# The unit matrix of a chunk's transition: added by the tensor engine in the accumulation, with the copy-out on the scalar engine

## The chip, the cores and the metric

One core of a Trainium2 chip runs the whole program. The metric is the device time of one execution in microseconds (us). PE is the tensor engine, DVE the vector engine, ACT the scalar engine, POOL the general one, SP the one that issues most loads; each has its own queue of instructions and they meet only at semaphores.

## What is computed

The reference is one layer of a streaming encoder over 512 prompt tokens and 32 sample tokens. One of its two mixing branches is a scan with a 64x64 matrix state for each of 8 heads:

```python
def step(s, inp):
    r_t, d_t, k_t, v_t, kk_t, b_t = inp
    sa = jnp.einsum('bhvk,bhk->bhv', s, -kk_t)
    s = (s * d_t[:, :, None, :] + sa[..., None] * b_t[:, :, None, :]
         + v_t[..., None] * k_t[:, :, None, :])
    return s, jnp.einsum('bhvk,bhk->bhv', s, r_t)
```

The kernel doesn't step token by token. For a chunk of 64 tokens (32 for the sample) the state goes over as a matrix product, S_new = (S E + update), scaled by the decay at the chunk's end. E = I + (a 64x64 product of two token-by-64 matrices) is the chunk's transition, and this case is about how its I comes in.

## The kernel before

All matrix products are in f32. The large projections ("dense", line 892) are cut into blocks of 128 output columns; each step of a block is three products (high and low parts of weights and activations), each over two halves of 272 tokens, into one of two PSUM buffers dense0 and dense1. The order of all work is one list, `SCHEDULE`; every engine walks through it and does its own share of each step, so that each engine's order is the list's order.

The scan runs over 5 tiles t: four of 128 tokens (two chunks each) and, as t = SAMPLE = 4, one of 32 tokens (one chunk). A tile is done for two groups g of four heads; c is the pair of heads, p the half of the 128 partitions that a head of the pair has. Small results share a ring of four PSUM banks, side0 to side3: the n-th filling takes bank n % 4, and PE may start it only when the filling four before it has been drained (`open_bank`, `drained`).

In a tile the steps that matter here are, in order of the list: `wu` (PE, line 818; ACT copies the result to `wu`, line 1275), `e` (PE, line 829; DVE adds I and writes `ebd`, line 1638), one piece of dense work of 12 products as filler, and then the next tile's triangular inversion (`wt` line 944 with ACT's copy to `xt` at 1285, `wm` line 744, `wd` line 758), woven with this tile's state update (`chain0` and `chain1`, lines 839, 840 and 844, which read `ebd`; DVE drains them to `mbd`, line 1646) and with the last tile's normalisation (line 1064 and others). In the sample's tile the filler between `wu` and `e` is a piece too. The gate filler of some tiles ends a block; then ACT applies tanh from dense0 or dense1 to `gst` (line 1401) and issues a store (line 1404). The tanh needs another ACT table than the square root at line 1318, so there is a table load where the two alternate.

Step `e` before: for each chunk one bank is filled by four products, one per head, `wu` transposed times `tok`; a bank is a 2x2 arrangement of 64x64 results. With K = 64 rows (the chunk's tokens) and 64 columns each product uses a quarter of PE's array: the rows of partitions 0-63 or 64-127 by the chunk, the columns 0-63 or 64-127 by p. In the sample's tile the products have K = 32.

DVE drains a bank with two instructions, one for each half of the partitions, each 64 partitions by 128 elements, with the unit matrix of the constants (`cst`, columns K_I64 on) as second operand of the addition.

Of the kernel before, what the change touches and what calls it, by code (L numbers as in the profile page):

```python
# [14 lines left out]
P = 128  # L15
# [329 lines left out]
def encoder_kernel(nc, i_, o_):  # L345
# [225 lines left out]
    def chunks(t):  # L571
        return [(c, CHUNK) for c in range(2)] if t < SAMPLE else [(0, DEC)]
# [158 lines left out]
    def wkv_pe(pe, step, transposes, close):  # L731
# [41 lines left out]
        if st == "tok":  # L773
            transposes(step, "t0", [((2 * q + c) * P, C[:, blk + 2 * g + c, 1 + j0:1 + j0 + n])
                                    for q, blk in enumerate((CR, CK)) for c in range(2)])
            transposes(step, "t1", [(c * P, C[:, CV + 2 * g + c, 1 + j0:1 + j0 + n]) for c in range(2)]
                       + [((2 + c) * P, AR[:, 2 * g + c, 0, j0:j0 + n]) for c in range(2)])
        elif st == "sb0":
            if t == 0:
                pe.wait_ge(s_["rw_done"], 2 * g + 2)  # L780
            w = 2 * B32 if nb > 1 else B32
            for p in range(2):
                b = open_bank(pe, step, f"b{p}")
                lo, hi = 64 * p, 64 * p + 64
                for c in range(2):
                    for q in range(nb):
                        i0 = j0 + 32 * q
                        ins = pe.matmul(b[32 * q:32 * q + 32, c * 64:c * 64 + w], C[lo:hi, CR + 2 * g + c, 1 + i0:1 + i0 + B32],
                                        AR[lo:hi, 2 * g + c, 0, i0:i0 + w], start=True, stop=True)
                close(ins, step, f"b{p}")  # L790
        elif st in ("sb1", "sk"):
            f, blk, us = ("r", CR, slice(1, 2)) if st == "sb1" else ("k", CK, slice(0, 2))
            m = n * (us.stop - us.start)
            for p in range(2):
                b = open_bank(pe, step, f"{f}{p}")
                lo, hi = 64 * p, 64 * p + 64
                for c in range(2):
                    ins = pe.matmul(b[0:n, c * m:(c + 1) * m].rearrange("p (u i) -> p u i", i=n),  # L798
                                    C[lo:hi, blk + 2 * g + c, 1 + j0:1 + j0 + n], AR[lo:hi, 2 * g + c, us, j0:j0 + n],
                                    start=True, stop=True)  # L800
                close(ins, step, f"{f}{p}")
        elif st == "gv":
            b = open_bank(pe, step, "gv")
            landed(pe, ("w", "tok", t, g), "t1")
            landed(pe, ("w", "sk", t, g), "k0")
            landed(pe, ("w", "sk", t, g), "k1")
            for h in range(4):
                ins = pe.matmul(b[0:n, h * 64:(h + 1) * 64], gt[0:n, g, h, 0:n], tok[0:n, g, 2, h, :], start=True, stop=True)  # L808
            close(ins, step, "gv")
        elif st == "wu":  # L810
            b = open_bank(pe, step, "wu")
            if nb > 1:
                landed(pe, ("wd", last_lv, t, g), "d")
            else:
                pe.wait_ge(s_["x64_set"], g + 1)
            landed(pe, ("w", "gv", t, g), "gv")
            for h in range(4):
                ins = pe.matmul(b[0:n, h * P:(h + 1) * P], xt64[0:n, g, h, 0:n],  # L818
                                ag[0:n, g, h, :, :].rearrange("p u v -> p (u v)"), start=True, stop=True)
            close(ins, step, "wu")  # L820
        elif st == "e":
            landed(pe, ("w", "wu", t, g), "wu")
            landed(pe, ("w", "tok", t, g), "t0")
            for ch, ln in chunks(t):
                b = open_bank(pe, step, f"e{ch}")
                r0, r1 = 64 * ch, 64 * ch + ln
                for c, p in heads:
                    h = 2 * c + p
                    ins = pe.matmul(b[64 * p:64 * p + 64, c * 64:(c + 1) * 64], wu[r0:r1, g, h, 0, :], tok[r0:r1, g, 0, h, :],
                                    start=True, stop=True)  # L830
                close(ins, step, f"e{ch}")
        elif st in ("chain0", "chain1"):
            ch = int(st[-1])
            r0, r1 = 64 * ch, 64 * ch + chunks(t)[ch][1]
            b = open_bank(pe, step, "c")
            for c, p in heads:
                h = 2 * c + p
                out = b[64 * p:64 * p + 64, c * P + 64 * p:c * P + 64 * p + 64]
                pe.matmul(out, tok[r0:r1, g, 0, h, :], wu[r0:r1, g, h, 1, :], start=c == 0, stop=False, skip_group_check=c > 0)  # L839
                pe.matmul(out, tok[r0:r1, g, 1, h, :], tok[r0:r1, g, 2, h, :], start=False, stop=True, skip_group_check=c > 0)  # L840
            landed(pe, ("w", "e", t, g), f"e{ch}")
            state_landed(pe, t, ch, g)
            for c in range(2):
                ins = pe.matmul(b[:, c * P:(c + 1) * P], ebd[:, g, ch, c, :], mbd[:, g, ch, c, :], start=False, stop=True,  # L844
                                skip_group_check=True)
            close(ins, step, "c")
        elif st == "q":
            b = open_bank(pe, step, "q")
            for p in range(2):
                landed(pe, ("w", "sb1", t, g), f"r{p}")  # L850
            for c, p in heads:
                h = 2 * c + p
                ins = pe.matmul(b[64 * p:64 * p + 64, c * n:(c + 1) * n], wu[0:n, g, h, 0, :], rb[0:n, g, h, 0:n],
                                start=True, stop=True)
            close(ins, step, "q")
        elif st == "ya":


            b = open_bank(pe, ("w", "yb", t, g), "y")
            for c, p in heads:  # L860
                h = 2 * c + p
                out = b[64 * p:64 * p + 64, c * n:(c + 1) * n]
                pe.matmul(out, wu[0:n, g, h, 1, :], rb[0:n, g, h, 0:n], start=c == 0, stop=False,
                          skip_group_check=c > 0)
                pe.matmul(out, tok[0:n, g, 2, h, :], gt[0:n, g, h, P:P + n], start=False, stop=True,
                          skip_group_check=c > 0)
        elif st == "yb":

            b = bank(step, "y")
            landed(pe, ("w", "q", t, g), "q")  # L870
            for ch, ln in chunks(t):
                state_landed(pe, t, ch, g)
                for c in range(2):
                    ins = pe.matmul(b[:, c * n + 64 * ch:c * n + 64 * ch + ln], mbd[:, g, ch, c, :],  # L874
                                    qT[:, g, c, 64 * ch:64 * ch + ln], start=False, stop=True, skip_group_check=True)
            close(ins, step, "y")
# [222 lines left out]
    def _(act):  # L1099
# [19 lines left out]
        for step in SCHEDULE:  # L1119
# [141 lines left out]
            elif k == "w":  # L1261
# [8 lines left out]
                elif st == "gv":  # L1270
                    b = full_bank(act, step, "gv")
                    drain(f_act(ag[0:n, g, :, 1, :], b[0:n, 0:256].rearrange("p (h v) -> p h v", h=4), ACT.Copy), step, "gv")
                elif st == "wu":
                    b = full_bank(act, step, "wu")
                    drain(f_act(wu[0:n, g, :, :, :].rearrange("p h u v -> p (h u v)"), b[0:n, 0:512], ACT.Copy, scale=-1.0),
                          step, "wu")
                elif st == "yb":
                    b = full_bank(act, step, "y")
                    drain(f_act(AR[:, 2 * g:2 * g + 2, 1, j0:j0 + n], b[:, 0:2 * n].rearrange("p (c i) -> p c i", c=2),
                                ACT.Copy), step, "y")  # L1280
# [148 lines left out]
    def _(dve):  # L1429
# [27 lines left out]
        for step in SCHEDULE:  # L1457
# [146 lines left out]
            elif k == "w":  # L1604
# [19 lines left out]
                elif st == "sk":  # L1624
                    mask = cst[0:n, K_SC:K_SC + 2 * P].rearrange("p (u i) -> p u i", u=2)[:, :, 0:n]
                    mask = mask.unsqueeze(1).broadcast_to([n, 2, 2, n])
                    for p in range(2):
# [1 line left out]
                        o = gt[0:n, g, p::2, :].rearrange("p c (u i) -> p c u i", u=2)[:, :, :, 0:n]  # L1629
                        drain(vec.tensor_tensor(o, b[0:n, 0:4 * n].rearrange("p (c u i) -> p c u i", c=2, u=2), mask,  # L1630
                                                ALU.mult), step, f"k{p}")
                elif st == "e":
                    for ch, ln in chunks(t):
                        b = full_bank(dve, step, f"e{ch}")
                        for p in range(2):
                            lo, hi = 64 * p, 64 * p + 64
                            i64 = cst[lo:hi, K_I64:K_I64 + 64].unsqueeze(1).broadcast_to([64, 2, 64])
                            ins = vec.tensor_tensor(ebd[lo:hi, g, ch, :, lo:hi], b[lo:hi, 0:P].rearrange("p (c k) -> p c k", c=2),
                                                    i64, ALU.add)
                        drain(ins, step, f"e{ch}")  # L1640
                elif st in ("chain0", "chain1"):

                    ch = int(st[-1])
# [196 lines left out]
```

## Time and profile before

| | |
|---|---|
| time before, median of 3 runs | 1107.36 us (1107.15 to 1109.85) |
| the profiled execution | 1107.29 us, of which the trace's span is 1105.5 us |
| PE busy | 1011.3 us, 91% of the span |
| DVE / ACT / POOL busy | 501.0 / 276.5 / 490.8 us |
| mean granted PE clock | 0.969 of full speed |

The scan with its fillers lies between about 355 and 565 us; before it are the input projections and attention, after it the output projections and the feed-forward part, which PE fills almost without a gap. The profile counts an f32 product as two weight loads (PEld) and two matmuls (PE), so that "x16" at line 829 is eight products. The form "64*64" beside a matmul is rows by columns of the array that its weights take. Matmuls overlap in the record: a group's duration reaches to the end of its last one, and the next group may have begun by then.

### The profile page before, as it was taken

The page shows a single profiled execution, that of the slowest core. Times are in us where ns is not written, and L with a number is a line of the kernel's source. Part 1 is how long each engine was busy: PE and PEld are TensorE (multiplying, and loading weights), DVE is VectorE, ACT ScalarE, POOL GpSimd, SP SyncE. Part 2 cuts the span into 40 slices and gives each one's busy share as a digit, 9 for nine tenths or more (in the row PEclk, how much of TensorE's full clock was granted, in tenths as well). Part 3 has the DMA queues.
Part 4 walks back from the last instruction along what each step waited for, and adds up shares of the span by engine and source line. Part 5 has one row for each costly group of instructions (what it writes and reads, how often), then busy time and mean ns, then how long its engine had stood idle before and what let it go on. Part 6 is the DMA issues. An engine that isn't in the chain of part 4 may idle for free.

```text
span 1105.5 us, 21747 instructions
## 1 busy us (share of the span) xinstructions
PE 1011.3 (91%) x8886; PEld 954.9 (86%) x8886; DVE 501.0 (45%) x859; ACT 276.5 (25%) x768; POOL 490.8 (44%) x327
## 2 busy tenths in 40 slices
PE   4999998899958889989989994999999999999995
PEld 4999998887856777768789994999999999999994
DVE  5566798367565555554348317232332333200003
ACT  4223452255421222423221235110110111010111
POOL 3555564323233113142164550555655556556561
PEclk9999999999979999999999996999999999999997
DMA  8233323422212100002412531233232332332232
GB/s 240 72 90 83 77 77 97 120 59 70 78 60 60 35 2 31 31 13 75 156 49 71 183 95 39 58 94 88 83 95 77 94 89 81 88 89 85 74 86 82
DMA packets 137580, 89.15 MB, mean 81 GB/s; under 512 B 5242, under 2 KB 129504, under 8 KB 137504
## 3 DMA queue, kind: packets, MB, share of 16 engines
q1 hardware_dynamic: 128356, 70.42, 22.5%
q10 hardware_dynamic: 9148, 17.65, 4.5%
q8 instruction: 56, 0.92, 0.4%
q14 instruction: 20, 0.16, 0.0%
HBM read 78.86 MB, written 9.19 MB: 80 GB/s over the span
## 4 chain that ended last, share of the span: by engine, by line
PE 80%; DVE 12%; ACT 2%; issue 2%; POOL 1%; DMA 1%; DVEq 0%; ACTq 0%; POOLq 0%
PE dense L892 64%; PE side L944 4%; PE side L844 1%; PE side L818 1%; PE side L1064 1%; PE side L987 1%; PE side L874 1%; PE side L808 1%; PE side L1013 1%; DVE amax L1509 1%; DVE mb L1803 1%; PE side L839 1%; PE side L798 1%; DVE gain L1452 1%; DVE otok L1536 1%
## 5 line engine op out<-in xcount | busy, mean ns | idle before, releaser
L647 POOL TENSOR_SCALAR w_hi<-w_raw 128x1024 fp32r<-128x1024 f32 x127 | 139.2, 1096 | 484.5 <-PE dense L892 467.0
L650 POOL TENSOR_TENSOR w_lo<-w_raw,w_hi 128x1024 fp32r<-128x1024 f32 x127 | 311.7, 2455 | 10.6
L892 PE MATMUL dense<-h_hi,w_hi 128*128 128x272 f32 x1392 | 306.3, 298 | 10.1 <-DVE h_lo L1445 8.5
L892 PE MATMUL dense<-h_lo,w_hi 128*128 128x272 f32 x1392 | 296.1, 290 | 0.0
L892 PE MATMUL dense<-h_hi,w_lo 128*128 128x272 f32 x1392 | 294.9, 289 | 0.0
L892 PEld LDWEIGHTS dense<-h_hi,w_hi 128*128 128x128 f32 x1392 | 222.9, 191 | 20.1 <-DVE h_lo L1445 9.6
L892 PEld LDWEIGHTS dense<-h_lo,w_hi 128*128 128x128 f32 x1392 | 224.3, 191 | 0.0
L892 PEld LDWEIGHTS dense<-h_hi,w_lo 128*128 128x128 f32 x1392 | 223.4, 191 | 0.0
L892 PE MATMUL dense<-S,w_hi 128*128 128x272 f32 x960 | 162.0, 291 | 1.7 <-DVE S L1806 1.5
L892 PEld LDWEIGHTS dense<-S,w_hi 128*128 128x128 f32 x960 | 136.5, 189 | 2.5 <-DVE S L1806 2.0
L892 PE MATMUL dense<-S,w_lo 128*128 128x272 f32 x480 | 99.5, 289 | 0.0
L1720 DVE TENSOR_TENSOR z<-side,gain 128x512 f32<-128x512 f32 x16 | 11.1, 692 | 175.2 <-ACT h_lo L1332 175.2
L892 PEld LDWEIGHTS dense<-S,w_lo 128*128 128x128 f32 x480 | 75.5, 188 | 0.0
L1777 DVE SCALAR_TENSOR_TENSOR S<-z,S 128x544 f32 (+1 forms) x22 | 53.7, 2442 | 22.4 <-ACT S L1371 22.4
L1772 DVE TENSOR_TENSOR z<-z,dense 128x544 f32<-128x544 f32 x22 | 15.9, 722 | 97.1 <-PE dense L892 97.1
L1421 ACT ACTIVATE zT<-dense 128x544 f32<-128x544 f32 x16 | 10.0, 625 | 157.0 <-PE side L944 134.8
L1371 ACT ACTIVATE S<-z 128x544 f32 (+1 forms) x22 | 14.5, 658 | 132.2 <-DVE z L1772 132.2
L1768 DVE SCALAR_TENSOR_TENSOR z<-z,dense 128x544 f32<-128x544 f32 x22 | 15.9, 721 | 58.7 <-ACT z L1367 58.7
L1367 ACT ACTIVATE z<-dense 128x544 f32<-128x544 f32 x22 | 13.7, 624 | 99.6 <-PE dense L892 99.6
L1167 ACT ACTIVATE qkv<-side,amax 128x128 f32<-128x128 f32 (+4 forms) x40 | 20.0, 500 | 42.3 <-DVE amax L1510 41.2
L704 POOL TENSOR_TENSOR AR<-AR 128x256 f32<-128x256 f32 (+1 forms) x10 | 6.9, 685 | 44.0 <-DVE AR L1697 44.0
L1658 DVE TENSOR_TENSOR gain<-side,cst 128x256 f32<-128x256 f32 (+1 forms) x40 | 13.5, 376 | 21.1 <-PE side L744 21.0
(249 smaller groups left out, 1314.9 us busy)
## 6 DMA issues: line engine op xcount, KB each, us to landing
w_raw<-in_w_ffn_in SPq DMA_DIRECT2D x44, 512.0 KB, 3.8
w_raw<-in_w_in SPq DMA_DIRECT2D x43, 512.0 KB, 3.9
w_raw<-in_w_ffn_out SPq DMA_DIRECT2D x16, 448.0 KB, 3.6
gates<-gst ACTq DMA_DIRECT2D x16, 272.0 KB, 2.0
w_raw<-in_w_o SPq DMA_DIRECT2D x8, 512.0 KB, 3.8
w_raw<-in_w_ffn_out SPq DMA_DIRECT2D x8, 512.0 KB, 3.7
mb<-gates ACTq DMA_DIRECT2D x1, 2176.0 KB, 8.8
ga<-gates ACTq DMA_DIRECT2D x1, 2176.0 KB, 9.4
```

Of the source, the lines that this page charges most:

```text
L647: nc.gpsimd.tensor_scalar(w_hi[:, slot, :], w_raw[:, slot, :], 1.0, 0.0, ALU.mult, ALU.add).then_inc(hi_split, 1)
L650: nc.gpsimd.tensor_tensor(w_lo[:, slot, :], w_raw[:, slot, :], w_hi[:, slot, :].bitcast(F32), ALU.subtract).then_inc(w_split, 1)
L892: ins = pe.matmul(acc[:, hf, 0:HALF], w, r[:, hf * HALF:(hf + 1) * HALF], start=first and n == 0, stop=final and n == 2)
L944: ins = pe.transpose(b[0:m, c0:c0 + n], src, ident[0:n, 0:n])
L1167: drain(f_act(probs[0:n, pb, m, 0:keys], b[0:n, 0:keys], ACT.Exp, bias=amax[0:n, 2 * pb + m:2 * pb + m + 1], scale=SCALE, accum_out=asum[0 ...
L1367: f_act(f_t.rearrange("p (a b) -> p a b", a=2), pa[:, :, 0:HALF], ACT.Tanh, scale=0.5).then_inc(s_["f_tanh"], 1)
L1371: f_act(dst, f_s.unsqueeze(1), ACT.Copy, scale=0.5).then_inc(s_["f_hi"], 1)
L1658: drain(vec.tensor_tensor(mce[:, g, 0:nb, :].rearrange("p b (h j) -> p b h j", h=4), src, mask.unsqueeze(1).broadcast_to([P, nb, 4, 16]), ...
L1720: drain(vec.tensor_tensor(z[:, 0:4, i * P:(i + 1) * P], bank(step, "z0")[:, 0:512].rearrange("p (t n) -> p t n", t=4), gi.unsqueeze(1).bro ...
L1768: vec.scalar_tensor_tensor(out=fs2, in0=ft2, scalar=1.0, in1=dps[sa][:, :, 0:HALF], op0=ALU.add, op1=ALU.mult).then_inc(dense_read[sa], 1)
L1772: vec.tensor_tensor(fs2, fs2, dps[sb_][:, :, 0:HALF], ALU.mult).then_inc(dense_read[sb_], 1)
L1777: vec.scalar_tensor_tensor(out=lo, in0=f_s.unsqueeze(1), scalar=0.5, in1=hi.bitcast(F32), op0=ALU.mult, op1=ALU.subtract).then_inc(s_["f_l ...
```

## The change

Step `e` only. On PE each of the four products of a bank is now preceded by a product of the unit matrix with itself into the same 64x64 place (start=True), and the old product accumulates on it (start=False). ACT copies the bank to `ebd` with two plain copies of 64 partitions by 128 elements; DVE has no part in the step any more.

```diff
                 for c, p in heads:
                     h = 2 * c + p
-                    ins = pe.matmul(b[64 * p:64 * p + 64, c * 64:(c + 1) * 64], wu[r0:r1, g, h, 0, :], tok[r0:r1, g, 0, h, :],
-                                    start=True, stop=True)
+                    out = b[64 * p:64 * p + 64, c * 64:(c + 1) * 64]
+                    i64 = cst[64 * ch:64 * ch + 64, K_I64:K_I64 + 64]
+                    pe.matmul(out, i64, i64, start=True, stop=False)
+                    ins = pe.matmul(out, wu[r0:r1, g, h, 0, :], tok[r0:r1, g, 0, h, :], start=False, stop=True)
                 close(ins, step, f"e{ch}")
...
+                elif st == "e":
+                    for ch, ln in chunks(t):
+                        b = full_bank(act, step, f"e{ch}")
+                        for p in range(2):
+                            lo, hi = 64 * p, 64 * p + 64
+                            ins = f_act(ebd[lo:hi, g, ch, :, lo:hi], b[lo:hi, 0:P].rearrange("p (c k) -> p c k", c=2), ACT.Copy)
+                        drain(ins, step, f"e{ch}")
...
-                elif st == "e":
-                    for ch, ln in chunks(t):
-                        b = full_bank(dve, step, f"e{ch}")
-                        for p in range(2):
-                            lo, hi = 64 * p, 64 * p + 64
-                            i64 = cst[lo:hi, K_I64:K_I64 + 64].unsqueeze(1).broadcast_to([64, 2, 64])
-                            ins = vec.tensor_tensor(ebd[lo:hi, g, ch, :, lo:hi], b[lo:hi, 0:P].rearrange("p (c k) -> p c k", c=2),
-                                                    i64, ALU.add)
-                        drain(ins, step, f"e{ch}")
```

The rank of the unit product is 64 in every tile (`cst` rows 64 ch to 64 ch + 63), also in the sample's, where the product that follows it has 32 rows. In the changed kernel lines 818 and before keep their numbers; the unit product is line 831, the old one 832, and what was at 839, 840, 844, 892, 944 and 1064 is at 841, 842, 846, 894, 946 and 1066. On ACT, 1275 is 1277, the new copy is 1284, 1285 is 1294 and 1401 is 1410.

PE, tile t = 2, the end of step `wu` and both groups' step `e`; before (side is a PSUM bank, x4 are four products in a row):

```order
1473 L818 MATMUL side2<-ag,xt64 128x128 x4
1474 L818 MATMUL side3<-ag,xt64 128x128 x4
1475 L829 MATMUL side0<-tok,wu 64x64 x4
1476 L829 MATMUL side1<-tok,wu 64x64 x4
1477 L829 MATMUL side2<-tok,wu 64x64 x4
1478 L829 MATMUL side3<-tok,wu 64x64 x4
1479 L892 MATMUL dense0<-h_hi,w_hi 128x272 x2
```

The same place after, the first of the four banks whole:

```order
1529 L818 MATMUL side2<-ag,xt64 128x128 x4
1530 L818 MATMUL side3<-ag,xt64 128x128 x4
1531 L831 MATMUL side0<-cst 64x64
1532 L832 MATMUL side0<-tok,wu 64x64
1533 L831 MATMUL side0<-cst 64x64
1534 L832 MATMUL side0<-tok,wu 64x64
1535 L831 MATMUL side0<-cst 64x64
1536 L832 MATMUL side0<-tok,wu 64x64
1537 L831 MATMUL side0<-cst 64x64
1538 L832 MATMUL side0<-tok,wu 64x64
```

Each product is now a pair into one place, a unit product and the old one, and nothing else stands at another place on PE.

ACT, the same tile, from the copy of `wu` to the next tile's first `xt`; before:

```order
369 L1275 ACTIVATE wu<-side2 128x512
370 L1275 ACTIVATE wu<-side3 128x512
371 L1401 ACT_TABLE_LOAD
372 L1401 ACTIVATE gst<-dense0,pvh 128x544
373 L1404 DMA gates<-gst 128x544
374 L1285 ACTIVATE xt<-side0 128x128
375 L1285 ACTIVATE xt<-side1 128x128
```

And after:

```order
377 L1277 ACTIVATE wu<-side2 128x512
378 L1277 ACTIVATE wu<-side3 128x512
379 L1284 ACTIVATE ebd<-side0 64x2x64 x2
380 L1284 ACTIVATE ebd<-side1 64x2x64 x2
381 L1284 ACTIVATE ebd<-side2 64x2x64 x2
382 L1284 ACTIVATE ebd<-side3 64x2x64 x2
383 L1410 ACT_TABLE_LOAD
384 L1410 ACTIVATE gst<-dense0,pvh 128x544
385 L1413 DMA gates<-gst 128x544
386 L1294 ACTIVATE xt<-side0 128x128
387 L1294 ACTIVATE xt<-side1 128x128
```

The eight copies stand between the copy of `wu` and the table load for the gate's tanh, which is behind them now; in the tiles 0, 1 and 3 they stand directly ahead of `xt`.

## Rows read from the trace of the kernel before

**Rows 1.** The page: shares of the chain that ended last, by engine.

```profile
PE 80%; DVE 12%; ACT 2%; issue 2%; POOL 1%; DMA 1%; DVEq 0%; ACTq 0%; POOLq 0%
```

**Rows 2.** The chain that ended last, tile 1: start us, us, what.

```profile
409.65 0.48 PE side L829 x16
410.13 1.71 PE dense L892 x12
```

**Rows 3.** Timeline, tile 1: start, us, engine, line, out<-in, count, idle before and releaser.

```profile
408.90 0.47 PE L829 MATMUL side<-tok,wu 64*64 64x64 f32 x16
409.00 0.60 ACT L1275 ACTIVATE wu<-side 128x512 f32<-128x512 f32 x1 [0.30 <-PE side L818]
409.39 2.46 DVE L1638 TENSOR_TENSOR ebd<-side,cst 64x128 f32<-64x128 f32 x8 [3.33 <-PE side L829]
409.65 0.48 PE L829 MATMUL side<-tok,wu 64*64 64x64 f32 x16 [0.28 <-ACT wu L1275]
410.06 0.52 PE L892 MATMUL dense<-h_hi,w_hi 128*128 128x272 f32 x2
...
411.43 0.42 PE L892 MATMUL dense<-h_hi,w_lo 128*128 128x272 f32 x2
...
411.68 0.38 PE L944 MATMUL side<-ident,xp 128*128 128x128 f32 x2
411.99 0.45 ACT L1285 ACTIVATE xt<-side 128x128 f32<-128x128 f32 x2 [2.39 <-PE side L944]
...
412.00 0.34 PE L839 MATMUL side<-wu,tok 64*64 64x64 f32 x4
...
412.16 0.29 PE L840 MATMUL side<-tok 64*64 64x64 f32 x4
...
412.39 0.33 PE L840 MATMUL side<-tok 64*64 64x64 f32 x4
...
412.65 0.71 PE L844 MATMUL side<-mbd,ebd 128*128 128x128 f32 x4
...
413.40 0.42 DVE L1646 TENSOR_TENSOR mbd<-side,pend 128x256 f32<-128x256 f32 x1 [1.55 <-PE side L844]
```

**Rows 4.** Groups by line, 340 to 560 us: DVE's additions, and ACT copies of their form.

```profile
L1638 DVE TENSOR_TENSOR ebd<-side,cst 64x128 f32<-64x128 f32 x36 | 10.4, 289 | 21.2 <-PE side L829 20.5
...
L1303 ACT ACTIVATE dtmp<-side 64x128 f32<-64x128 f32 x2 | 0.5, 271 | 7.7 <-PE side L944 6.0 <-DMA out_wkv_prompt<-dtmp 1.8
```

**Rows 5.** Timeline, the sample's tile.

```profile
544.14 0.83 PE L829 MATMUL side<-tok,wu 32*64 32x64 f32 x16
...
544.90 0.52 PE L892 MATMUL dense<-o_hi,w_hi 128*128 128x272 f32 x2
```

**Rows 6.** Timeline, PE, tile 3: from 128 to 32 rows of the array.

```profile
504.90 0.41 PE L892 MATMUL dense<-h_hi,w_lo 128*128 128x272 f32 x2
505.24 0.31 PE L944 MATMUL side<-ident,xp 32*128 32x32 f32 x2
```

**Rows 7.** Timeline, tile 2, ACT's queue and what PE does.

```profile
456.98 1.28 ACT L1401 ACT_TABLE_LOAD   x1
...
459.23 0.71 ACT L1401 ACTIVATE gst<-dense,pvh 128x544 f32<-128x544 f32 x1 [0.97 <-PE dense L892]
...
460.35 0.45 ACT L1285 ACTIVATE xt<-side 128x128 f32<-128x128 f32 x2 [0.40 <-ACT gst L1401]
...
460.64 0.43 PE L744 MATMUL side<-gain,wa 128*32 128x64 f32 x16
...
461.00 1.14 PE L1064 MATMUL side<-AR,cst 128*128 128x256 f32 x4
```

**Rows 8.** PE in stretches: us, PE busy (count), granted clock, DMA share, GB/s.

```profile
428.00:432.00 4.00, 3.65 (x33) 0.57 0.02 4
...
492.00:496.00 4.00, 2.24 (x18) 1.00 0.01 2
541.00:545.00 4.00, 4.00 (x31) 0.57 0.10 36
```

## The prediction

> **What bounds the kernel now.** I read the page first: 80% of the chain that ended last is PE's and 12% DVE's [rows 1]. That makes PE's own time dear and DVE's cheap, but it is an average, so the second look is at the chain at step e. There it goes from PE's products of e (the second group) straight into 1.71 us of dense filler, with no DVE in between [rows 2]. The third look is the timeline of the same place, which shows why. DVE starts its eight additions at 409.39 and ends them at 411.85. The first reader of their result, the 128-row product at line 844, starts at 412.65 and follows the line 840 ahead of it; DVE itself then stands idle for 1.55 us before its next instruction [rows 3]. So the addition on DVE is not waited for, and DVE gets nothing urgent behind it. What the change saves is off the path; what it adds to PE is on it.
>
> **Term 1: DVE's part goes.** 36 additions of 289 ns, 10.4 us of DVE's time [rows 4]. In tile 1 they end 0.80 us before line 844 starts, and the DVE instruction that follows them waits for PE for 1.55 us [rows 3]; the sample's tile has the same filler behind e, from 544.90 on [rows 5]. I take 0. If DVE had something to start there, a saving could be at most the additions' 2.46 us a tile, but its idle time behind them speaks against any.
>
> **Term 2: the unit products in the four large tiles.** PE gets 8 more products for each group of a tile, 64 in four tiles. How long does a pair last, unit product and old one, both into the same place of the same quarter of the array? Line 829 is no measure for that, since its products go to other quarters in turn: 8 products in 0.41 us, from 409.65 to the next work at 410.06. The state update at lines 839 and 840 has exactly this form: pairs into one place, 64*64, the place changing with each pair. Its four pairs start at 412.00 and the next work starts at 412.65; the two groups of line 840, of two products each, start 0.23 us apart, so a pair has a period of about 0.12 us, and the last pair with the change to the 128*128 form takes 0.17 us more than its period [rows 3]. A group of e has 8 pairs: 8 x 0.12 = 0.96 us to the next product of the same form, and 0.96 + 0.17 = 1.13 us to other work.
> The two groups don't cost the same. The first starts at 408.90 and the second can't start before ACT has copied wu, at 409.65, which leaves slack behind the first. With 0.96 us the first reaches 409.86: 0.21 us late. The second then takes 1.13 us in place of 0.41: 0.72 us more. Together 0.93 us a tile, and 3.7 us for four. The filler behind it is PE's own work and gives nothing back, and all later waits of PE for DVE or ACT in the tile are for work that PE itself feeds later.
> Low end: the pairs run at line 829's pace, twice 0.41 us: the first group would reach 409.72 (0.07 late), the second takes 0.41 more, 0.48 a tile, 1.9 in all. High end: each four pairs take the whole 0.65 us: 1.30 a group, 0.55 + 0.89 = 1.44 a tile, 5.8 in all.
>
> **Term 3: the sample's tile.** Here a group has four pairs (eight in all), both groups run one behind the other, and the old product has 32 rows while the unit product has 64: the array's form changes at each of the 16 products. The 8 products take 0.76 us now, from 544.14 to 544.90, part of it at the lower clock [rows 5, 8]. What does a change of rows alone cost? From a dense group of two to line 944 in the same form it is 411.43 to 411.68, 0.25 us [rows 3]; where line 944 has 32 rows it is 504.90 to 505.24, 0.34 us [rows 6]. So a change costs about 0.09 us more; the 0.17 us at line 844 is another view of it, with the columns changing too. A product whose partner uses the same quarter takes 0.12 us, with the change 0.21; 16 x 0.21 = 3.4 us, less 0.76, gives 2.6 us. No matmul in the trace goes from 64 to 32 rows at the same columns and back, so the ends are wide: without a cost of the change 8 x 0.12 + 0.17 - 0.76 = 0.4 us; with 0.15 us for each change at full clock 16 x 0.27 - 0.76 = 3.6, and up to 5 us if half of it falls under the lower clock that this place has before [rows 8]. The value is taken from the row-only change, the nearest row.
> The Trainium skill, "TensorEngine Tiling (Array Packing)", section "Key Properties", says that a change of the tiling mode, and not just of the tile, drains the engine; the extra 0.09 us of [rows 6] agrees with it in kind. By that rule this term exists, and if a unit product of 64 rows and a product of 32 rows were one mode after all, the term would be its low end.
>
> **Term 4: ACT's part.** ACT gets 36 copies of 64x128 at 271 ns [rows 4], 9.8 us in all. In tile 1 eight of them start when the copy of wu ends, 409.60, and last 2.2 to 2.4 us, to about 412.0, the later banks coming from PE just in time. What is queued behind them is xt at 411.99, and its input comes from PE at about 0.9 us later than now [rows 3], so nothing waits: 0 in tiles 0, 1 and 3. In tile 2 the table load for the gate's tanh is behind the copies. Now it runs at 456.98, under the filler, ahead of the tanh at 459.23, and xt follows at 460.35 [rows 7]. After: copies to about 459.3, table to 460.6, tanh to 461.3, store issue and gap 0.4 as now, xt of the first group done at about 461.95 and of the second at 462.2. PE waits for both, since the second half of line 744 and line 1064 take the banks that these two copies free. By term 2 PE would come to them at about 461.7 and 461.9 (460.64 and 461.00 plus 0.93, the former plus half its length) [rows 7], so it stands for about 0.3 us. Ends: 0 if PE is later by the high end of term 2, 0.8 if it is later by its low end.
>
> **Sum.** 0 + 3.7 + 2.6 + 0.3 = 6.6 us. The profiled execution took 1107.29 us, 1.8 more than its span and 0.07 less than the median of the runs, so 1107.3 + 6.6 = 1113.9 us. The low ends give 1.9 + 0.4 + 0.8 = 3.1 us, 1110.4; the high ends 5.8 + 5.0 + 0 = 10.8 us, 1118.1.
>
> **The clock.** After some stretches in which PE partly stood idle its granted clock is at the lower of its two levels (1.2 in place of 2.4 GHz) for a while: the mean from 428 to 432 is 0.57, one of four such stretches between 400 and 480, and a fifth is at 541. At 492, with PE busy for only 2.24 of 4 us, it stayed at 1.00 [rows 8]. At a mean of 0.57 a busy stretch of 4 us does 2.3 us of work, so such a fall costs about 1.7 us. Which of them come when all moves by a microsecond I can't tell from the rows. I expect as many as before; one more or less is the rest of the uncertainty.
>
> **The rivals.** (a) The change of rows is free in the sample's tile: terms 2 and 4 with 0.4, 4.4 us, 1111.7 us. For it: no row shows the change between 64 and 32 rows at the same columns; against it: 128 to 32 rows does cost [rows 6]. (b) The pairs overlap as line 829's products do, and the sample's tile pays nothing: 3.1 us, 1110.4, and with one fall of the clock fewer 1108.7, within 0.3%. Against it: the four pairs of lines 839 and 840 take 0.65 us where eight products of line 829 take 0.41 [rows 3]. (c) One fall of the clock more, after an idle stretch like that at 492: 1113.9 + 1.7 = 1115.6, with two 1117.3. (d) Faster: the falls of the clock go. If the four between 400 and 480 fail to come, as one after 492 did, that gives back 4 x 1.7 = 6.8 us, which beats the added work from the point where this costs less than 3.5 us, as in (b): 1107.3 + 3.1 - 6.8 = 1103.6 us. The mechanism is real, but it needs every fall to go and the low ends together; nothing in the change shortens PE's idle stretches, which come from DVE's work in the inversion.
>
> **Chances.** The forecast 0.45, (a) 0.23, (b) 0.13, (c) 0.15, (d) 0.04. A measurement of this kernel can tell about 0.3% (3.3 us) from no change, so slower means above 1110.7 and faster below 1104.0. The forecast, (a) and (c) are slower, 0.83, and 0.01 of (b) is; the rest of (b), 0.12, is the same; (d), 0.04, is faster. The range runs from the lower half of (b) with no fall of the clock gone, 1109.5, to the high ends, 1118.0, which leaves out (d), a part of (b) and two more falls on top of the high ends.
>
> **What would show each step.** DVE's busy time falls by 10.4 us and ACT's rises by about 9.8, with no change of the path by either. In tile 1 the first e group to the second should be 0.96 us instead of 0.75, and the second to the filler 1.13 instead of 0.41; 0.82 in each would be (b)'s pace. In the sample's tile the unit products and the old ones should last 3.4 us from the first to the filler, with the matmuls' starts 0.2 us apart; about 1.1 us is (a). In tile 2 the table load should start at about 459.3 plus what has been lost by then, and lines 746 or 1066 should show a wait of about 0.3 us for ACT. PE's mean clock should stay near 0.97. I'd be wrong if PE pulled unit products ahead into the wait for ACT's wu (they stand behind that wait in PE's queue, so they can't), if DVE's idle time behind the additions turned out to be a wait that its own lateness caused, or if the clock fell more often.

## The result and the profile after

The changed kernel is slower by 0.66% of the time before, as forecast: ratio 1.0066 with a 95% interval of 1.0051 to 1.0082 (7 runs of each; medians 1116.01 and 1109.85 us, 6.2 apart). By the ratio that is 7.3 us more; 6.6 had been forecast. Measured again later (e12_after_again, 6 runs) it was 1.0083 (1.0055 to 1.0111), 9.2 us. The profiled execution took 1115.65 us with a span of 1113.9, against 1107.29 and 1105.5 before.

The page's busy times and chain shares of the changed kernel, beside [rows 1]:

```profile
PE 1020.0 (92%) x9030; PEld 962.3 (86%) x9030; DVE 490.3 (44%) x823; ACT 286.1 (26%) x804; POOL 490.1 (44%) x327
PE 80%; DVE 12%; ACT 3%; issue 2%; POOL 1%; DMA 1%; DVEq 0%; ACTq 0%; POOLq 0%
```

DVE lost 10.7 us of busy time, ACT gained 9.6, PE 8.7. The chain's shares hardly moved: the page alone doesn't tell what happened.

Tile 1 in the timeline of the changed kernel, the place of [rows 3] (line 831 is the unit product, 832 the old one, 894 the dense filler, 1284 ACT's copy):

```profile
410.73 0.34 PE L831 MATMUL side<-cst 64*64 64x64 f32 x4
...
410.84 0.60 ACT L1277 ACTIVATE wu<-side 128x512 f32<-128x512 f32 x1 [0.30 <-PE side L818]
...
410.90 0.29 PE L832 MATMUL side<-tok,wu 64*64 64x64 f32 x4
...
411.02 0.33 PE L831 MATMUL side<-cst 64*64 64x64 f32 x6
...
411.49 0.27 PE L831 MATMUL side<-cst 64*64 64x64 f32 x1
...
411.50 2.29 ACT L1284 ACTIVATE ebd<-side 64x128 f32<-64x128 f32 x8
...
412.19 0.33 PE L832 MATMUL side<-tok,wu 64*64 64x64 f32 x4
...
412.45 0.52 PE L894 MATMUL dense<-h_hi,w_hi 128*128 128x272 f32 x2
...
414.36 0.45 ACT L1294 ACTIVATE xt<-side 128x128 f32<-128x128 f32 x2 [0.57 <-PE side L946]
...
414.37 0.34 PE L841 MATMUL side<-wu,tok 64*64 64x64 f32 x4
```

From the first product of e to the filler it is 1.72 us (410.73 to 412.45); before it was 1.16. The second group still starts 0.76 us after the first (411.49), 0.05 us after ACT's copy of wu ends at 411.44, as before, so the first group's eight added products are hidden whole; the second takes 0.96 us in place of 0.41. ACT's copies are done 0.57 us before xt's input comes. Tiles 0, 2 and 3 have the same 1.71 to 1.72 us.

Tile 2, the place of [rows 7], where a table load is behind the copies now:

```profile
456.78 2.29 ACT L1284 ACTIVATE ebd<-side 64x128 f32<-64x128 f32 x8
...
457.73 0.52 PE L894 MATMUL dense<-h_hi,w_hi 128*128 128x272 f32 x2
...
459.09 1.28 ACT L1410 ACT_TABLE_LOAD   x1
...
460.39 0.71 ACT L1410 ACTIVATE gst<-dense,pvh 128x544 f32<-128x544 f32 x1
...
461.51 0.45 ACT L1294 ACTIVATE xt<-side 128x128 f32<-128x128 f32 x2 [0.41 <-PE side L744]
461.84 0.32 PE L744 MATMUL side<-gain,wa 128*32 128x64 f32 x8 [0.57 <-ACT xt L1294]
462.10 1.13 PE L1066 MATMUL side<-AR,cst 128*128 128x256 f32 x4
...
463.15 0.43 PE L758 MATMUL side<-gain,xt 128*32 128x64 f32 x16
```

PE stands 0.57 us for ACT's xt, as the chain of banks foretold, and gets to line 758 5.42 us after the filler's start (463.15 less 457.73); before it was 4.65 (457.42 to 462.07). That is 0.77 us.

The sample's tile, the place of [rows 5]; of 16 rows, one for each product, the first, the last at the full clock and those around the fall are shown:

```profile
546.12 0.32 PE L831 MATMUL side<-cst 64*64 64x64 f32 x2
546.37 0.32 PE L832 MATMUL side<-tok,wu 32*64 32x64 f32 x2
...
548.91 0.32 PE L832 MATMUL side<-tok,wu 32*64 32x64 f32 x2
549.17 0.47 PE L831 MATMUL side<-cst 64*64 64x64 f32 x2
549.57 0.47 PE L832 MATMUL side<-tok,wu 32*64 32x64 f32 x2
...
550.76 0.82 PE L894 MATMUL dense<-o_hi,w_hi 128*128 128x272 f32 x2
```

Here the products stand apart: each starts 0.25 us after the one before (3.05 us for twelve), and 0.40 us at the lower clock (1.59 us for the last four). Together 4.64 us in place of 0.76. It is the largest single part of the loss. And the clock, the stretches of [rows 8] in the changed kernel (us, PE busy and count, granted clock, DMA share, GB/s):

```profile
428.00:432.00 4.00, 2.37 (x27) 1.00 0.00 0
448.00:452.00 4.00, 3.73 (x31) 1.00 0.00 0
477.00:481.00 4.00, 4.00 (x37) 0.57 0.02 4
...
535.00:539.00 4.00, 4.00 (x27) 0.57 0.66 186
...
549.00:553.00 4.00, 4.00 (x20) 0.51 0.00 0
553.00:557.00 4.00, 4.00 (x29) 0.63 0.00 0
```

Two falls of the four between 400 and 480 are gone (428, 448), one has come at 535, and the one at 541 is now a double one from 549 to 556.

Since a single fall of the clock shifts a whole time by 1 to 2 us, the stages are compared with their falls named. The table gives, for each trace, the us from one tile's first product of e to the next tile's, the last column from the sample's to the first dense product that reads y; in brackets the us of full clock that PE was not granted in the stage (its windows of 1 us, 1 less the granted clock; one fall is 1.7). The labels are those of the experiments below.

| | tile 0 to 1 | 1 to 2 | 2 to 3 | 3 to sample | sample to y |
|---|---|---|---|---|---|
| before | 40.21 (1.7) | 47.35 (3.4) | 46.13 (1.7) | 41.76 (1.5) | 37.30 (0.2) |
| after | 40.85 (1.7) | 45.29 (0) | 47.45 (1.7) | 42.65 (1.7) | 43.54 (3.4) |
| e12_after_again | 40.95 (1.7) | 47.93 (3.4) | 45.86 (0) | 42.52 (1.6) | 43.60 (3.5) |
| e1_sample_old | 40.93 (1.7) | 47.92 (3.4) | 45.87 (0) | 42.46 (1.6) | 37.16 (0.1) |
| e11_large_again | 40.83 (1.7) | 45.29 (0) | 47.46 (1.7) | 42.63 (1.7) | 37.14 (0.1) |
| e3_no_unit | 39.31 (0) | 44.73 (0) | 47.29 (1.7) | 41.51 (1.2) | 37.62 (0.5) |
| e10_no_unit_t2 | 40.35 (1.7) | 46.33 (1.7) | 44.54 (0) | 41.96 (1.6) | 37.20 (0.1) |

Where two traces do the same work and have their falls at the same places (after and e11_large_again, e12_after_again and e1_sample_old, each up to the sample) the stages agree within 0.06 us; with a fall elsewhere in the stage they differ by up to 0.17 (42.46 and 42.63). The kernel before alone has 1107.39 to 1112.35 us in 27 runs. Part of that comes from where the programs are alike: from the start to the first tile's e the traces have 368.2 (e9_hoisted_wide) to 373.0 us (e12_after_again), 368.7 before and 369.9 after. In this table the change can be read, in the whole time only its sum. For before and after the sums of the five stages are 212.75 and 219.78 us, 7.03 more, and by chance each has 8.5 us not granted.

### The profile page after: what moved, and what is told of

Read it like the earlier page. It is cut to its first block, busy times and chain, and to the rows that moved or that the text cites. A ratio compares the mean times of both kernels' runs of the same rounds, so it can differ in the third digit from the quotient of the medians.

```text
span 1113.9 us, 22035 instructions
## 1 busy us (share of the span) xinstructions
PE 1020.0 (92%) x9030; PEld 962.3 (86%) x9030; DVE 490.3 (44%) x823; ACT 286.1 (26%) x804; POOL 490.1 (44%) x327
## 4 chain that ended last, share of the span: by engine, by line
PE 80%; DVE 12%; ACT 3%; issue 2%; POOL 1%; DMA 1%; DVEq 0%; ACTq 0%; POOLq 0%
PE dense L894 63%; PE side L946 4%; PE side L846 1%; PE side L1066 1%; PE side L818 1%; PE side L876 1%; PE side L989 1%; PE side L808 1%; PE side L1015 1%; DVE amax L1518 1%; DVE mb L1803 1%; PE side L841 1%; DVE gain L1461 1%; DVE otok L1545 1%; PE side L798 1%
## 5 line engine op out<-in xcount | busy, mean ns | idle before, releaser
L1646 DVE TENSOR_TENSOR mbd<-side,pend 128x256 f32<-128x256 f32 x18 | 7.6, 424 | 43.0 <-PE side L846 43.0
```

## The experiments

Theory 1: the added time is PE's own, term by term (large tiles, sample, ACT's late table in tile 2). The rivals: it is the falls of the clock that any shift brings, or ACT's added load everywhere, or the number of products and not their change of form.

**The large tiles alone** (e1_sample_old, and the same program as e11_large_again):

```diff
+                    if t < SAMPLE:
+                        pe.matmul(out, i64, i64, start=True, stop=False)
-                    pe.matmul(out, i64, i64, start=True, stop=False)
...
+                    ins = pe.matmul(out, wu[r0:r1, g, h, 0, :], tok[r0:r1, g, 0, h, :], start=t == SAMPLE, stop=True)
```

and in the sample's tile DVE adds as before.

> The sample's tile does step e as before (no unit product, DVE adds), the four large tiles as in the changed kernel. Theory 1 (the added time is PE's: 0.56 us a large tile, 3.9 us in the sample's tile because the array's form changes at each product, and about 0.9 us from ACT's later table load in tile 2): e in the sample's tile is back at 0.5 to 0.8 us, and the time is the kernel before plus 3.1 us (2.2 + 0.9), ratio about 1.003. Theory 2 (the added time is mostly falls of PE's clock that came with the shift, not the products): the sample's tile gets short, but the time stays near plus 7 us, ratio 1.0066.

Measured: 1.0064 (1.0047 to 1.0081, 4 runs), which is theory 2's number and a miss of theory 1's. The trace says otherwise: with the falls of e12_after_again, the changed kernel, up to the sample, all stages but the last are equal to it within 0.06 us, and the last is 37.16 in place of 43.60. Of the 5.5 us by which this trace is longer than that of the kernel before, 3.7 lie ahead of the first tile's e (372.4 against 368.7 us), where nothing was changed. So it was run again:

> The same program as e1_sample_old, unit products and ACT's copy in the large tiles only, measured again because its ratio, 1.0064 from 4 runs, is at odds with e4_rows32 (1.003 from 10 runs), which differs from it by 0.4 us of work. Theory 1: 3.3 us, ratio 1.003. If 1.006 comes again, the falls of the clock cost this program 3 us in a way that its neighbours are spared.

Measured: 1.0016 (0.9998 to 1.0033, 12 runs). This trace has the falls of the first trace of the changed kernel up to the sample, its stages equal it within 0.02 us, and then 37.14 stands against 43.54. The two times of one program, on two chips, lie further apart than their intervals allow; the 3.0 us of the stages (2.2 for e and 0.8 for tile 2's table, 1.0027) lie between. The mean granted clock goes with it: 0.961 over the first four runs (0.967 in the kernel before beside them), 0.967 over the twelve (0.965 beside them). The large tiles' part is settled by the stages, not by these two times.

**The sample's tile alone** (e8_sample_only), the opposite condition on both edits:

> The counterpart of e1_sample_old: only the sample's tile has the unit products and ACT's copy, the four large tiles are as before. Theory 1 (products whose row count changes each time, 0.25 us each at the full clock, and their sparse use of PE brings one or two falls of the clock behind them, as in the traces with them): e in the sample's tile lasts 4.0 to 5.0 us, from there to the first output product 41 to 44 us in place of 37.3, the time is the kernel before plus 4 to 6 us, ratio 1.0036 to 1.0055. Theory 2 (the added time is falls of the clock that any of the changes brings, wherever it is): the ratio is the same 1.006 to 1.007 as with only the large tiles changed. If the parts add up (1.0064 for the large tiles alone, 1.0066 for both), this one would be 1.000: then the sample's tile would cost nothing.

Measured: 1.0042 (1.0025 to 1.0058), 4.7 us, with e of the sample 4.41 us and 43.05 us from there to y. Theory 1; theory 2's 1.006 to 1.007 lies outside. In after and e11_large_again the last stage is 6.4 us longer than with the old way (43.54 to 37.14), of which 4.0 are e itself (4.64 to 0.61 us) and 2.4 come with the double fall that begins in it.

**The same number of products without the change of form** (e4_rows32):

```diff
-                    i64 = cst[64 * ch:64 * ch + 64, K_I64:K_I64 + 64]
+                    i64 = cst[r0:r1, K_I64:K_I64 + 64]
```

> The changed kernel, but the sample's unit product has 32 rows like the product behind it, so the array's form doesn't change between the two; half of the unit matrix is left out of the sample's E. As many products as in the changed kernel. Theory 1: e in the sample's tile lasts 1.0 to 1.3 us in place of 4.64, and the time is the changed kernel minus 3.5 to 5 us: ratio to the kernel before 1.002 to 1.0035. If it is the number of products and not the change of form: 4.6 us and ratio 1.0066.

Measured: 1.0030 (1.0012 to 1.0048), and the sample's e in its timeline:

```profile
547.31 0.34 PE L831 MATMUL side<-cst 32*64 32x64 f32 x4
547.47 0.29 PE L832 MATMUL side<-tok,wu 32*64 32x64 f32 x4
...
548.17 0.33 PE L832 MATMUL side<-tok,wu 32*64 32x64 f32 x4
548.43 0.52 PE L894 MATMUL dense<-o_hi,w_hi 128*128 128x272 f32 x2
```

Sixteen products in 1.12 us in place of 4.64, and the last stage is 37.71 us. Only the rows of the unit product's weights differ, and where all have 64 rows, in the large tiles, sixteen take 0.96 us. So it is the change between 64 and 32 rows that costs: 0.25 us for a product with it, 0.07 (1.12 us by sixteen) without. The rows of the weight loads (PEld) of the changed kernel and of this run show what else is different:

```profile
546.37 0.19 PEld L832 LDWEIGHTS side<-tok,wu 32*64 32x64 f32 x2
...
547.42 0.20 PEld L832 LDWEIGHTS side<-tok,wu 32*64 32x64 f32 x4
```

With the change (first line) the load starts together with its product (546.37), without it 0.05 us ahead (547.42 and 547.47), beside the products that go before. The Trainium skill, "TensorEngine Tiling (Array Packing)", "Key Properties", says that a change of mode drains the engine; this pair of runs agrees in kind.

**Unit products first** (e5_units_first): in a group all unit products stand ahead of all old ones.

```diff
+                for c, p in heads:
+                    pe.matmul(b[64 * p:64 * p + 64, c * 64:(c + 1) * 64], i64, i64, start=True, stop=False,
+                              skip_group_check=True)
+            for ch, ln in chunks(t):
+                b = bank(step, f"e{ch}")
...
+                    ins = pe.matmul(out, wu[r0:r1, g, h, 0, :], tok[r0:r1, g, 0, h, :], start=False, stop=True,
+                                    skip_group_check=True)
```

> The changed kernel, but within a group all unit products come first and all old ones behind them, so that neighbours go to different quarters of the array and the sample's tile has 4 changes of form in place of 16. Theory 1: the second group of a large tile goes from 0.95 us to 0.65 to 0.75, the sample's e from 4.64 to 1.3 to 1.6 us; the time is the changed kernel minus 4 to 5.5 us, ratio 1.0015 to 1.003. If what counts is the number of products alone: no change.

Measured: 1.0024 (1.0010 to 1.0037), within the forecast. In this form part of E comes out without its unit matrix, since one unit product follows another into the same partitions with start=True (see the end); the work is the same. The large tiles' e went from 1.72 to 1.43 us (the second group to 0.67) and the sample's to 2.48, above the forecast, since it fell wholly under the lower clock; its timeline shows the four blocks:

```profile
546.73 0.69 PE L828 MATMUL side<-cst 64*64 64x64 f32 x8
547.36 0.69 PE L836 MATMUL side<-tok,wu 32*64 32x64 f32 x8
547.97 0.69 PE L828 MATMUL side<-cst 64*64 64x64 f32 x8
548.60 0.69 PE L836 MATMUL side<-tok,wu 32*64 32x64 f32 x8
```

Four products and one change of form take 0.62 us at the lower clock, where two changes of form with one product each took 0.80. Same products, other order: the ratio is 0.0042 lower than the changed kernel's 1.0066, 4.7 us, and the intervals don't meet.

**The unit products twice in the large tiles** (e6_units_twice, the second overwrites the first):

> In the large tiles each unit product is made twice (the second overwrites the first), so that a place gets three products in place of two; the sample's tile is as in the changed kernel. Theory 1, products of one place wait for each other at about 0.11 us each: the second group of e goes from 0.95 to about 1.45 us and the first no longer fits into the wait for wu (0.75 us), so the stretch from the first e product to the filler is 2.4 to 2.8 us in place of 1.72; the time is the changed kernel plus 2.8 to 4.3 us, ratio to the kernel before 1.009 to 1.0105. A rival (the products overlap and their issue alone counts, about 17 ns a record): stretch 2.0 us, ratio 1.0075.

Measured: 1.0115 (1.0098 to 1.0132), with e at 3.08 us in each large tile. That is 1.36 us more for 16 more products, above the forecast of up to 1.1 us more, and the time is above its range too: 5.4 us more than the changed kernel, as 4 x 1.36 asks. Since now the first group no longer fits into the wait for wu, every added product counts in full. The rival of mere issue (2.0 us) is out.

**DVE makes the copies** (e2_dve_copy) and **no unit product, ACT copies** (e3_no_unit): the two halves of the change, one at a time.

> Unit products on PE as in the changed kernel, but DVE makes the plain copies and ACT has no part in step e. Theory 1: PE doesn't wait for ACT's xt in tile 2 any more (0.57 us of wait gone, and about 0.9 us between e and line 758 there), the e stretches stay at 1.72 us in the large tiles and 4.6 in the sample's; the time is the kernel before plus 6.1 us, ratio 1.0055. A rival (what slows the kernel is ACT's added load everywhere, not the products): ratio below 1.002.

> ACT copies e out, but no unit product is made and none added: the unit matrix is left out of E. This is the move from DVE to ACT by itself. Theory 1: the e stretch of a large tile is 1.16 us as before, the sample's 0.5 to 0.8; only tile 2 has the table load behind the copies, and PE's wait for xt there, which now meets a PE that comes 0.56 us earlier than in the changed kernel: about 1.1 us. The time is the kernel before plus 1.1 us, ratio 1.001. The rival of ACT's load: ratio 1.004 or more.

Measured: e2_dve_copy 1.0067 (1.0049 to 1.0086), e 1.71 to 1.72 us in the large tiles; no wait for xt at line 744; its stage from tile 2 to 3 is 46.10 (1.7), against 47.45 (1.7) of the changed kernel, though its fall lies elsewhere in the stage. The rival (below 1.002) is out; the wait of tile 2 that is gone, 0.0007 of the time, is too little for the ratio to show. The trace is that of the longest of its four executions: its sample's tile lies in five falls on end (8.3 us not granted, e 6.40 us). e3_no_unit 1.0026 (1.0013 to 1.0038), more than expected: with e at 1.16 to 1.17 us as before, PE's waits for ACT in its trace have

```profile
PE side L744 <- ACT xt L1292: 0.9, 1, 0.9
```

where the changed kernel has 0.6, since PE comes 0.55 us earlier to a table that is no earlier; and the stage from tile 2 to 3 is 47.29, against 46.13 before with a fall at the same place. So the late table costs 1.2 us by itself; the 1.7 us above that in the ratio are not explained. Whether ACT's copies cost elsewhere, the next one asks.

**The same, but DVE copies in tile 2** (e10_no_unit_t2):

> As e3_no_unit (no unit matrix in E at all, ACT copies), but in tile 2 DVE makes the copies, so that ACT's table load and tanh start early again. Theory 1: the 1.0026 of e3_no_unit was tile 2's late table, 1.2 us of 46, and the rest is chance in the falls of the clock; now the stage from tile 2's e to tile 3's is 46.1 us again with one fall of the clock (47.3 in e3_no_unit), ratio 1.000 to 1.001. Theory 2 (ACT's copies cost in every tile): ratio stays at 1.0015 to 1.0026.

Measured: 0.9991 (0.9978 to 1.0003), and the wait for xt at line 744 is not in the trace. Theory 2 is out: ACT's copies are free in the tiles where no table load stands behind them, and DVE's additions were free before, since taking them away (all but tile 2's copies) gave nothing that can be told from zero. It had no fall from tile 2 to 3, so nothing stands beside the expected 46.1 with one; its 44.54 stands against 45.87 without a fall in e1_sample_old, which has the late table and the unit products: 1.33 us, as 0.55 and 0.77 ask. The step from e3_no_unit's ratio, 0.0035, is more than the 1.2 us of the table (0.0011); the rest goes with the scatter.

**What the theory would build**: the unit products ahead of the wait for wu, tile 2's copies on DVE, the sample's tile as before (e7_hoisted), and the same with one unit product of 128 columns for each half of a bank (e9_hoisted_wide). The part of the edit that concerns PE, as it is in e9_hoisted_wide:

```diff
+            landed(pe, ("w", "tok", t, g), "t0")
+            if t < SAMPLE:
+                for ch, ln in chunks(t):
+                    b = open_bank(pe, step, f"e{ch}")
+                    i64 = cst[64 * ch:64 * ch + 64, K_I64:K_I64 + 64]
+                    for p in range(2):
+                        pe.matmul(b[64 * p:64 * p + 64, 0:P].rearrange("p (c k) -> p c k", c=2), i64,
+                                  i64.unsqueeze(1).broadcast_to([64, 2, 64]), start=True, stop=False, skip_group_check=True)
             landed(pe, ("w", "wu", t, g), "wu")
-            landed(pe, ("w", "tok", t, g), "t0")
...
```

> What the theory would build: in the large tiles the unit products stand ahead of the wait for wu, where PE waits for ACT anyway, and the old ones behind it; in tile 2, where ACT's table load would be late, DVE makes the plain copies; the sample's tile is as before. Theory 1: from the end of wu's products (line 818) to the filler a large tile is at most 0.3 us longer than before (0 if the wait covers all), no wait for xt in tile 2, and the time is the kernel before plus 0 to 1.2 us, ratio 0.9995 to 1.0012. Rival (the clock's falls depend on any change in the tiles): ratio above 1.003. It can't be faster than before by more than noise, since DVE's additions were never waited for.

> As e7_hoisted (unit products of the large tiles ahead of the wait for wu, DVE's plain copies in tile 2, the sample's tile as before), but with one unit product of 128 columns for each half of a bank, 2 in place of 4, so that no unit product follows another into the same partitions with start=True. Theory 1: in the large tiles the stretch from the end of wu's products to the filler is that of before within 0.2 us; ratio 0.999 to 1.001, since DVE's additions were never waited for and ACT's copies aren't either. A rival (DVE's freed 9 us do help somewhere): ratio below 0.998.

Measured: e7_hoisted 0.9988 (0.9970 to 1.0006), no difference that can be told, in line with the forecast (it has e5_units_first's fault in E). From the start of wu's products to the filler a large tile takes 3.30 us, before 3.10, in the changed kernel 3.65; so 0.20 of 0.55 us are left. e9_hoisted_wide has 3.28 us, all stages to y together 213.6 us against 212.75 before, and a profiled execution of 1107.55 us, but 1.0053 (1.0032 to 1.0073) in its 10 runs, from 1107.55 to 1118.78. The miss is 5 us. The mean granted clock of its runs is 0.962, that of the kernel before beside it 0.965, which is in line with more falls and gives about 3 us (an estimate: 0.003 of 1110). The trace has one thing more: at line 798, between tile 3 and the sample, PE waits 2.6 us for ACT's `dtmp`, which waits for the store of the prompt's state, in place of 1.5 us in the other traces. But the longer of its runs have no trace, so where they lost their time, and why in this program, stays open. Neither beats the kernel before.

**The changed kernel once more**, beside the last three:

> The changed kernel itself, beside the three others on one chip. By the parts (large tiles alone 1.003 if e4_rows32 is right, the sample's tile alone 1.0042) it should be 1.0065 to 1.0075; if e1_sample_old's 1.0064 is right and the parts add up, 1.0105.

Measured: 1.0083 (1.0055 to 1.0111), between the two sums; the interval holds both, so it doesn't decide between them.

## Why the prediction held, and where its terms were off

The direction, the place and the size of the sum were right: 6.6 us forecast, 7.3 measured (interval 5.7 to 9.1), and the medians' 1116.01 lies in the range. The terms were right in kind, and the three that aren't 0 were each wrong in size: measured, they are 2.2 + 3.9 + 0.8 = 6.9 us. That the sum came so near is in part luck, since a term too high stood beside two too low, and falls of the clock that came cancelled others that went.

- **Term 1, DVE's part is worth nothing: right.** e10_no_unit_t2 takes it away and gains nothing (0.9991, the interval holds 1). DVE stands idle behind the place where its additions were.
- **Term 2, the large tiles: 3.7 us forecast, 2.2 measured** (4 x 0.55, shown by 1.71 against 1.16 us, and by 45.29 against 44.73 in the stage without falls of the changed kernel and e3_no_unit). The step that failed is the period of 0.12 us for a pair, taken from four pairs of one chunk and applied to all eight. In e the two chunks use different rows of the array, and the second chunk's pairs begin beside the first's: the row at 411.02 has six records where those of lines 839 and 840 have four, and the two more are the second chunk's, 0.29 us after the first chunk's start and not 0.48 (4 x 0.12). Eight pairs take at most 0.76 us to the next group and not 0.96, so the first group is hidden, and 0.96 us to the filler and not 1.13, so the second costs 0.55 more, not 0.72. That the slack of the wait for wu takes up the first group was right.
- **Term 3, the sample's tile: 2.6 us forecast, 3.9 measured** (4.64 less 0.76). The mechanism, a cost at each change of rows, was right and is shown by e4_rows32; the price of a product with a change was mis-sized, 0.21 us where 0.25 was measured (0.7 us over sixteen), and the last four products ran at the lower clock (0.6 us). By the single records of the two traces the step from one product to the next is 0.15 us with the change and 0.06 without, so that the 0.09 read from [rows 6] was right as far as it went. What it left out is inside the product: its second record starts 0.11 us after the first when a change stands ahead, 0.06 when none does, and line 944 was timed by its first alone. The higher end that stood beside the value (0.27 for a product) was nearer. The weight loads at line 944 show the same as those of e4_rows32: with equal rows the load starts 0.11 us ahead of its product at 411.68, with 32 rows only together with it (505.24).

```profile
411.57 0.26 PEld L944 LDWEIGHTS side<-ident,xp 128*128 128x128 f32 x2
...
505.24 0.20 PEld L944 LDWEIGHTS side<-ident,xp 32*128 32x128 f32 x2
```

- **Term 4, ACT in tile 2: 0.3 us forecast, 0.8 measured.** The chain of banks was right to the line (744 waits for xt). PE came 0.55 us late, not 0.93, and so waited longer; 0.3 + 0.38 gives 0.7.
- **The clock: as many falls as before, and in the first pair of traces it was so by luck** (8.5 us not granted in the five stages of each). Between tiles 1 and 2 two falls are gone, which gave back 2.6 us (47.35 + 0.55 - 45.29), and with the sample's tile two came, which cost 2.4. The latter are not neutral. From tile 3's e to y the five traces with the alternating products (after, e12_after_again, e8_sample_only, e2_dve_copy, e6_units_twice) have 3.9 to 8.9 us not granted, e5_units_first with its four changes 3.8, and seven with the old way there or with equal rows 1.7 to 2.0. The eighth of these, e9_hoisted_wide, has 5.3, so such falls can come without the alternating products; what brings them, no run shows. Rival (c) had a fall more behind an idle stretch; here PE was not idle in the record, but had one small product each 0.25 us. The terms with 2.4 us for these falls come to 9.3, which is above the 7.3 measured and near the 9.2 of e12_after_again.
- The price of a fall was 1.7 us by the rows' mean; between the two traces of the changed kernel, in stages that differ in their falls alone, it is 1.3 (47.93 less 45.29, for two) and 1.6 us (47.45 less 45.86).

## What to carry to other kernels

Before work is moved from an idle engine onto the one that sets the time, look at who waits for it: an operation whose engine stands idle behind it and whose reader comes later is free, and any price on the busy engine is too high. Small matmuls into quarters of the array took 0.05 to 0.07 us each next to each other, and over three times as much with a change of the number of rows between every two of them; put those of one form in a block, or give both the same rows. An engine that gets a new job ahead of a table load delays what stands behind the load; and where falls of the clock scatter the whole time by half a per cent, compare stages with the same falls.

## What the runs showed of the hardware

- A product of 64x64 weights and 64 columns between two of 32 rows starts 0.25 us after its neighbour at the full clock (0.40 at the lower), the same products with equal rows every 0.07 us (after, e4_rows32).
- In e5_units_first and e7_hoisted two unit products with start=True went into different columns of the same 64 partitions of a bank before either was accumulated on, and part of E lost its unit matrix; with one unit product for each half of the partitions (e9_hoisted_wide) it didn't. The old code's start=c == 0 in the state update keeps to the same rule. Which columns lose it, no run shows. The Trainium skill, "PSUM — Partial Sum Buffer", section "The four PSUM rules", says that the first product of an accumulation clears the marks of what has been written in the whole bank, for the partition quadrants that it reaches, and not in its own columns alone, so that a later accumulation into columns whose mark is gone overwrites them. That two runs lost part of it and one lost none agrees; by the Trainium skill's rule the quarters with c = 0 would lose the unit matrix.
- The same program, measured beside the same kernel before, gave 1.0064 and 1.0016 on two chips (e1_sample_old, e11_large_again), with intervals that don't meet, and the clock's falls lie at other places in the two traces. It isn't the chip alone: up to the sample the first has the falls of e12_after_again, which ran on the other chip. Stages with falls at the same places agree within 0.06 us.
